# Modulation chunks of a two-layer model: four in the head, twenty multiplied on GpSimd during the even mixer

## What is computed

```
def modulate(hn, shift, scale):
    return hn * (1 + scale[:, None, :]) + shift[:, None, :]
...
proj = h @ w_in
qa, ka, va, za, ba, aa, qb, kb, vb, qi, ki, wi = split_cols(proj, EVEN_SPLITS)
...
oa = gated_delta_rule(qa, ka, va, g, beta)
...
ob = dsa_sparse_attention(qb, kb, vb, qi, ki, wi)
o = jnp.concatenate([oa.reshape(b_, s_, -1), ob.reshape(b_, s_, -1)], axis=-1)
return o @ w_out
```

## Time and profile before

| | us |
|---|---|
| median of 3 runs | 2447.55 |
| lowest and highest | 2442.32, 2449.39 |
| the profiled execution | 2446.35 |
| its span | 2444.7 |
| TensorE busy in the span | 2013.4 (82%) |
| VectorE, ScalarE busy | 647.2, 338.2 |
| GpSimd busy | 7.8 |

### The profile page before, as it was taken

The page is one execution under the profiler, slowest core; times in us unless marked ns, Lnnn a source line. Parts: engine busy times, 40 slices in busy tenths (PEclk is TensorE's granted clock), DMA queues, the critical chain, the costliest instruction groups (busy, mean ns, idle before and its releaser), DMA issues. The chain is left out here.

```text
span 2444.7 us, 28446 instructions
## 1 busy us (share of the span) xinstructions
PE 2013.4 (82%) x11842; PEld 1277.8 (52%) x11842; DVE 647.2 (26%) x1485; ACT 338.2 (14%) x690; POOL 7.8 (0%) x12
## 2 busy tenths in 40 slices
PE   1999567699999997796569999999818999789987
PEld 0374464465555553363435655555407886548753
DVE  0133653222222222103721222222231222511082
ACT  0111211100000000101211111111001121300161
POOL 0000000000000000000000000000000000000000
PEclk9799688699999998697679999999959999999989
DMA  8934001299999999932017999999873434154200
GB/s 271 386 102 165 0 2 69 102 429 427 429 428 429 429 429 403 376 105 106 1 70 303 429 429 429 429 428 429 352 266 107 143 138 142 61 124 168 98 1 26
DMA packets 154570, 590.32 MB, mean 241 GB/s; under 512 B 40784, under 2 KB 48476, under 8 KB 129668
## 3 DMA queue, kind: packets, MB, share of 16 engines
q1 hardware_dynamic: 127136, 561.63, 57.7%
q10 hardware_dynamic: 26212, 23.51, 2.9%
q0 software_dynamic: 1152, 4.19, 0.5%
HBM read 571.42 MB, written 17.89 MB: 241 GB/s over the span
## 5 line engine op out<-in xcount | busy, mean ns | idle before, releaser
L1602 PE MATMUL bank<-ring,own_tokens 128*64 128x256 f32 x4096 | 469.2, 383 | 57.0 <-DMA ring<-in_exp_w_dram 54.0
L1602 PEld LDWEIGHTS bank<-ring,own_tokens 128*64 128x64 f32 x4096 | 304.1, 138 | 238.6 <-DMA ring<-in_exp_w_dram 99.0
L506 PE MATMUL bank<-hT,ring 128*128 128x256 f32 (+1 forms) x1552 | 338.7, 381 | 5.0 <-PEq L422 5.0
L506 PEld LDWEIGHTS bank<-hT,ring 128*128 128x128 f32 (+1 forms) x1552 | 294.2, 190 | 48.6 <-issue 6.8
L1622 PE MATMUL bank<-ring,own_hiddenT 128*64 128x512 f32 x1024 | 233.8, 597 | 3.8
L495 PE MATMUL bank<-ring,hT 128*128 128x512 f32 (+2 forms) x416 | 168.8, 567 | 0.0
L1718 DVE TENSOR_TENSOR own_hidden<-bank,own_silu 128x256 f32<-128x256 f32 x64 | 27.2, 425 | 482.7 <-ACT own_silu L1662 482.7
L1581 PE MATMUL bank<-xn_kept,member 128*64 128x512 f32 x528 | 128.0, 605 | 14.1 <-issue 14.1
L1622 PEld LDWEIGHTS bank<-ring,own_hiddenT 128*64 128x64 f32 x1024 | 75.8, 136 | 120.3 <-issue 120.3
L495 PEld LDWEIGHTS bank<-ring,hT 128*128 128x128 f32 x416 | 79.0, 190 | 88.1 <-issue 83.2
L1662 ACT ACTIVATE own_silu<-bank 128x256 f32<-128x256 f32 x64 | 24.6, 384 | 680.2 <-PE bank L1602 680.2
(11 more groups left out here) (511 smaller groups left out, 1787.4 us busy)
## 6 DMA issues: line engine op xcount, KB each, us to landing
ring<-in_exp_w_dram SPq DMA_DIRECT2D x192, 2048.0 KB, 21.8
ring<-in_ada_w_dram SPq DMA_DIRECT2D x24, 2048.0 KB, 20.0
ring<-in_hawk_w_in_dram SPq DMA_DIRECT2D x15, 2048.0 KB, 8.0
expert_out<-own_out ACTq DMA_DIRECT2D x128, 128.0 KB, 8.5
ring<-in_even_w_in_dram SPq DMA_DIRECT2D x7, 2048.0 KB, 17.5
ring<-in_gla_w_in_dram SPq DMA_DIRECT2D x6, 2048.0 KB, 20.0
ring<-in_nsa_w_in_dram SPq DMA_DIRECT2D x5, 2048.0 KB, 7.9
ring<-in_even_w_out_dram SPq DMA_DIRECT2D x2, 2048.0 KB, 8.2
```

Source lines behind the costliest of these rows:

```text
L506: last = nc.tensor.matmul(pair[m // 2][0:rows, (m % 2) * T:(m % 2 + 1) * T], w[:, k, m * P:m * P + rows], src[:, k, :], start=(k == 0), st ...
L1602: last = nc.tensor.matmul(bank[2 + q][halves[half], part * FE // 2:(part + 1) * FE // 2], own[:, q, k % 4, k // 4, :], w[:, k, cols], star ...
```

## The change

The list of chunks now begins with only four modulation chunks of layer 0 (shift and scale ahead of the mixer). The other 20 (`later`) are in the list between the eight chunks of the even projections, one behind each, and twelve more behind the last. `head_stage` replaces four blocks: it issues silu(c)'s own load first, makes norm and transposes beside the products of the four chunks, and writes hT. The vectors' tables come over GpSimd's queue, the router weights are loaded by ScalarE in the projection block.

The 20 later chunks are multiplied on GpSimd in place in the ring (`ada_products`): eight multiplications by a column of silu(c), then three adds that fold eight row tiles into one, into `ada_acc` (two buffers of two chunks). GpSimd takes 8 chunks in the projections, 3 in the attention, 2 in the norms, 5 in the levels, 2 in the outputs. TensorE adds over the partitions with columns of ones (`ada_sum`), VectorE adds the bias and the gain (`ada_keep`); there are ten such sums, at the places that the diff shows. A chunk's slot is freed by GpSimd (`ada_taken`). The expert block of layer 0 has no `following` any more; SyncE fills the ring to its end there. The projection block uses three pairs of PSUM banks instead of four, since banks 6 and 7 serve the sums.

```
-            group(f"ada{layer}")
-            for j in range(12):
-                cols_of(A["ada_w"][layer], 0, KD, [(512 * j, 512)])
             if layer == 0:
-                group("even_in")
+                group("ada_first")
+                for j in range(4):
+                    ada_chunk(0, j)
+                even_at = []
                 w = A["even_w_in"][0]
+                for n, parts in enumerate([[(c0, 512)] for c0 in (0, 512, 1024, 1536, 2056, 2568, 3080)] + [[(2048, 8), (3592, 324)]]):
+                    even_at.append(len(chunks))
+                    cols_of(w, 0, KD, parts)
+                    later_at.append(len(chunks))
+                    ada_chunk(*later[n])
+                for n in range(8, len(later)):
+                    later_at.append(len(chunks))
+                    ada_chunk(*later[n])
...
+        def head_stage(rowsA, rowsB):
...
+                        act.dma_start(silu_c[:, :], flat(A["c"]).rearrange("(k p) -> p k", p=P)).then_inc(c_in.up(16), 16)
+                        act.dma_start(x[:, :, :], A["x"][0].rearrange("(t p) d -> p t d", p=P)).then_inc(x_in.up(16), 16)
+                        act.dma_start(first_gain[:, :], A["norm_mix"][0].rearrange("(k p) -> p k", p=P)).then_inc(bias_in.up(16), 16)
+                        act.dma_start(ada_bias[:, 0, 0:2, :], A["ada_b"][0, 0:2 * D].rearrange("(q k p) -> p q k", p=P, k=KD)).then_inc(bias_in.up(16), 16)
+                        act.wait_ge(c_in.sem, c_in.at(16))
+                        nc.scalar.activation(silu_c[:, :], silu_c[:, :], ACT.Silu).then_inc(silu_ready.up(), 1)
...
+                        for j in range(4):
+                            if j == 3:
+                                pe.wait_ge(consts_in.sem, consts_in.at(16))
+                                pe.wait_ge(normed.sem, normed.at(TT))
+                                turn_tiles(pe, xn, turned)
...
+        def ada_products(pool, acc, n0, n1):
+
+            for n in range(n0, n1):
+                c = later_at[n]
+                dst = acc[:, (n // 2) % 2, n % 2, :]
+                if n % 2 == 0 and n >= 4:
+                    pool.wait_ge(ada_summed.sem, n // 2 - 1)
+                arrived(pool, c)
+                w = slot(c)
+                for k in range(KD):
+                    ins = nc.gpsimd.tensor_scalar(w[:, k, :], w[:, k, :], silu_c[:, k:k + 1], None, ALU.mult)
+                for k in (4, 2):
+                    ins.then_inc(ada_steps.up(), 1)
+                    pool.wait_ge(ada_steps.sem, ada_steps.n)
+                    ins = nc.gpsimd.tensor_tensor(w[:, 0:k, :], w[:, 0:k, :], w[:, k:2 * k, :], ALU.add)
+                ins.then_inc(ada_steps.up(), 1)
+                pool.wait_ge(ada_steps.sem, ada_steps.n)
+                ins = nc.gpsimd.tensor_tensor(dst, w[:, 0, :], w[:, 1, :], ALU.add)
+                ins.then_inc(ada_taken.up(), 1)
+
+        def ada_sum(pe, acc, n, banks):
+
+            kind = later[2 * n][1] // 2
+            pe.wait_ge(ada_taken.sem, 2 * n + 2)
+            if n:
+                pe.wait_ge(ada_kept.sem, n)
...
+                                      pairs=3, tensor_work={0: turn_tables, 2: sum_kind(0), 4: sum_kind(1), 6: sum_kind(2), 7: sum_kind(3)},
+                                      scalar_work={0: load_positions, 3: sines, 4: later_loads, 6: silu_conv}, vector_work=convolve_and_rotate,
+                                      pool_work=lambda pool: ada_products(pool, acc, 0, 8), at=even_at)
...
-        def experts_stage(layer, gates, xn, gain, shift, following):
+        def experts_stage(layer, gates, xn, gain, shift):
...
-                        if following:
-                            following[2](pe)
```

More of the change, by code:

```diff
@@ L68 @@
 C_ONES = C_IDENT + P
-C_TRIU = C_ONES + P
+C_PICK = C_ONES + P
+C_EARLY = C_PICK + 1
+C_TRIU = C_EARLY
 C_LEVEL = C_TRIU + P
@@ L397, in turn_tiles @@
+        router_in, bias_in = signal("router_in"), signal("ada_bias_in")
+        consts_in, tables_in = signal("consts_in"), signal("tables_in")
+        gates = [sb(st_first, f"gates{layer}", [P, 2, D]) for layer in range(2)]
+        mod = [sb(st_first, f"mod{layer}", [P, 4, KD]) for layer in range(2)]
         def turn_tiles(pe, src, per_bank):
@@ new lines, in ada_sum @@
+        def ada_sum(pe, acc, n, banks):
[3 more added lines that the diff above has]
+                pe.wait_ge(ada_kept.sem, n)
+            whole = acc[:, n % 2, :, :].rearrange("p h n -> p (h n)")
+            for k in range(KD):
+                if kind in (2, 5):
+                    if k < 2:
+                        last = nc.tensor.matmul(banks[k][:, :], ones, acc[:, n % 2, k, :], start=True, stop=True)
+                elif kind < 2:
+                    last = nc.tensor.matmul(banks[0][:, k:k + 1], whole[:, k * P:(k + 1) * P], ones[:, 0:1], start=True, stop=True)
+                else:
+                    for half in range(2):
+                        last = nc.tensor.matmul(banks[0][half * 64:half * 64 + 64, k:k + 1], acc[:, n % 2, half, k::KD], ones[:, 0:1], start=True, stop=True)
+            last.then_inc(ada_summed.up(), 1)
@@ new lines, in ada_keep @@
+        def ada_keep(dve, n, banks):
+            layer, kind = later[2 * n][0], later[2 * n][1] // 2
+            dve.wait_ge(ada_summed.sem, n + 1)
+            dve.wait_ge(bias_in.sem, bias_in.n)
+            if kind in (2, 5):
+                for h in range(2):
+                    g = gates[layer][:, kind // 3, h * 512:(h + 1) * 512]
+                    ins = nc.vector.tensor_tensor(g, banks[h][:, :], g, ALU.add)
+                ins.then_inc(ada_kept.up(), 1)
+                return
+            half, shift = kind // 3, kind % 3 == 0
+            row = mod[layer][:, 2 * half + (1 if shift else 0), :]
+            ins = nc.vector.tensor_tensor(row, banks[0][:, 0:KD], ada_bias[:, layer, 2 * half + kind % 3, :], ALU.add)
+            if not shift:
+                ins.then_inc(vector_steps.up(), 1)
+                dve.wait_ge(vector_steps.sem, vector_steps.n)
+                gain = ffn_gain[:, layer, :] if half else col("norm_mix", 8 * layer, KD)
+                ins = nc.vector.scalar_tensor_tensor(row, row, 1.0, gain, ALU.add, ALU.mult)
+            ins.then_inc(ada_kept.up(), 1)
@@ new lines, in load_tables @@
+        def load_tables(act):
+            for layer in range(2):
+                for half in range(2):
+                    act.dma_start(gates[layer][:, half, :], A["ada_b"][layer, (3 * half + 2) * D:(3 * half + 3) * D].partition_broadcast(P))\
+                        .then_inc(bias_in.up(16), 16)
+                act.dma_start(ada_bias[:, layer, 2:4, :], A["ada_b"][layer, 3 * D:5 * D].rearrange("(q p k) -> p q k", p=P, k=KD)).then_inc(bias_in.up(16), 16)
+            act.dma_start(ada_bias[:, 1, 0:2, :], A["ada_b"][1, 0:2 * D].rearrange("(q k p) -> p q k", p=P, k=KD)).then_inc(bias_in.up(16), 16)
+            act.dma_start(ffn_gain[:, :, :], A["norm_ffn"].rearrange("l (p k) -> p l k", k=KD)).then_inc(bias_in.up(16), 16)
```

394 lines of the change are left out of this document (215 added, 179 removed).

## The result

The changed kernel takes 2508.73 us (median of 4 runs, 2505.77 to 2509.68) against 2448.47 us of the kernel before in the same comparison: a ratio of 1.0249, with a 95% interval of 1.0228 to 1.0269. It is slower by 60 us where I forecast 49 us faster, and it lies above the range. The profiled execution took 2505.77 us, its span is 2504.1 us.

A forecast was written before the change was run, and what follows sets the result against it. Even-layer blocks were taken as chains of small VectorE and TensorE steps with GpSimd idle, head and tail as held by issues and modulation work. Plus 86, minus 78, minus 57 gave minus 49: forecast 2399 us, range 2338 to 2469.

The forecast's parts named there:

- GpSimd's price, 13.8 us a chunk: Even layer's blocks: VectorE's 7.64 us times 1.8 per modulation chunk on GpSimd, 276 us in all for 20 chunks.
- the upper bound of 18.3 us: GpSimd's price: the slowest elementwise row, the scan, at 2.4 ns a column times the 7,680 columns of a chunk.
- The sign that I had named for being wrong: More than 16 us from one chunk's first product to the next one's would show the forecast wrong.
- The interference, 57 us in full: Even blocks: GpSimd stands still for VectorE instructions working all in SBUF; 31 us in projections, 7, 4, 12.7, 2.5 elsewhere.
- Rival (d): Even blocks: GpSimd binds too strongly; change loses from 16.2 us a chunk, 2469 us at 17.3; 26 in 100.
- The head, minus 78: Before the first projection: silu(c) no longer behind router loads, eight chunks fewer; projections start at 47 instead of 125 us.
- Rival (c): Head: 4 B runs go slower or silu(c) waits behind issues; head gains only 55, 2422 us; 10 in 100.
- The tail, minus 57: Behind layer 0's experts: modulation work and late SyncE issue go; norm of layer 1 starts at 968.6 instead of 1025.6 us.
- Edits at nothing: Three bank pairs, router issues in the projections (up to 37 us of ScalarE), the ring and TensorE's new waits cost nothing extra.
- The sums: Even blocks: TensorE's additions over partitions; 3 us for the last in the projections, norms' two hidden under GpSimd.
- Rival (a): Even blocks: no interference between GpSimd and VectorE; blocks plus 29 in all, 2342 us; 15 in 100.
- Rival (b): Even blocks: GpSimd near VectorE's price, 7.6 to 10 us a chunk; 2327 us; 7 in 100.

The follow-up runs named there:

- wide_mul: Changed kernel with one GpSimd multiplication of 128x4096 by spread silu(c) instead of eight of 128x512 by a column; 2465.3 us, ratio 1.0073.
- scalar_mul: Changed kernel with ScalarE making the eight multiplications of every later chunk and GpSimd only adding; 2397.3 us, ratio 0.9796.
- half_mul: Changed kernel with four of the eight GpSimd multiplications of every later chunk left out; 2398.8 us, ratio 0.9798.
- mul_only: Changed kernel without GpSimd's adds of 128x2048 and 128x1024, all multiplications and the last add kept; 2376.5 us, ratio 0.9711.
- last_add_only: Changed kernel with only GpSimd's last add of 128x512 per later chunk kept, multiplications and two adds left out; 2347.0 us, ratio 0.9587.
- scalar_small_adds: ScalarE multiplies and GpSimd adds, with the two larger adds cut into pieces of 128x512, otherwise the changed kernel; 2385.2 us, ratio 0.9756.

## Why the prediction was wrong, point by point

**GpSimd's price, 13.8 us a chunk: this step failed.** An undisturbed chunk takes 20.65 us from its start to the next one's (412.63 to 433.28 us in the levels): 12.3 us of multiplications, 6.9 and 1.3 of adds. Two things were wrong in the working. The factor 1.8 came from one tiny MEMSET; for the adds it was nearly right (4.50 against 2.29 us), but the multiplication by a column is 3.8 times VectorE's 0.43 us. And the upper bound of 18.3 us was none: the slowest elementwise row of VectorE, 2.4 ns a column, says nothing of another engine, whose own row is 3.2. Twenty times 6.85 us are 137 us. The sign that I had named for being wrong, more than 16 us from one chunk to the next, is there. The Trainium skill (GPSIMD Engine Reference, section 3, Performance versus the Vector engine) gives 4,497 ns for the add of 2,048 columns, and the trace agrees with 4,505. By the Trainium skill's factor for that add the estimate would have been 15.0 us a chunk, also too low.

**The interference, 57 us in full: wrong in size and in place.** From the first to the last instruction of each block GpSimd took 431 us for 20 chunks, 18 more than 20 x 20.65. I had let GpSimd stand still for VectorE. It is mostly VectorE that is held: its busy time in the five blocks went from 114.7 to 158.9 us, and where GpSimd works with two tensors at a time it reaches 284 (wide_mul). In the changed kernel VectorE's part costs nothing that the rows show, since GpSimd sets every block; when GpSimd gets faster, it does (the projections of wide_mul, and part of the 43 us of scalar_mul). The two errors together: 137 - 39 = 98 of the 102 us by which the even blocks were mis-forecast.

**The shape of the argument held.** Barriers throw away any slack, each block lasts as long as its share of chunks, and every microsecond a chunk counts about 20 times: half_mul took 6.2 us a chunk away, 123 us in all, and gained 110. My figure at 13.8 us a chunk was 2399 us; half_mul, at 14.5 undisturbed, took 2398.8, and mul_only, at 13.7, 2376.5. That half_mul meets the figure is luck: its interference and its waits are not those of the sum. Rival (d) was the right case, but its price (17.3 us, 2469) was too low as well. Its turning point of 16.2 us a chunk fits half_mul and mul_only on the one side and the changed kernel on the other; wide_mul, at 15.3 undisturbed and slower than before, shows that the price alone doesn't decide.

**The head, minus 78: measured minus 72.** The chain was faster than I had it: the four issues ahead of silu(c) took 0.47, 0.60, 0.49 and 4.79 us, silu(c) came at 8.64 us, not near 22, and hT was written at 40.9. What I had as two SyncE issues until 48 us lasted until 52.4, and the barrier waited 11.5 us for them alone. Rival (c), short runs of 4 B holding silu(c), is refuted.

**The tail, minus 57: measured minus 56.7.** The norm follows the last copy after 27.47 us; I had 27.3. The 27 was a choice between two merges of before, 20.2 and 28.1 us, near the one with loads beside it.

**Edits at nothing.** The router's issues took 10.8 us in the projections instead of 37 in the head and cost nothing. Three pairs of banks cost nothing that the rows show. The waits of TensorE on GpSimd are real, 28.7 and 25.6 us, but they are GpSimd's lateness, not a cost of their own:

```profile
PE bank L516 <- PEq L1194: 40.4, 1, 40.4
PE bank L510 <- POOL ada_acc L497: 28.7, 1, 28.7
PE bank L516 <- POOL ada_acc L497: 25.6, 2, 13.2
```

The sums I had at 3 us in the projections and nothing to 4 elsewhere; without GpSimd's cover the five blocks are 28 us longer in all (last_add_only), of which the sums' own rows name 8.0 in the projections. **Rival (a)**, no interference, would have given 2342 us at 13.8 us a chunk; mul_only, at that price, with little interference, took 2376.5. The 34 us are in the projections (123.3 for 113), the attention (43.9 for 41.4), the norms (32.0 for 28), the levels (85.1 for 69.5, 10.3 of it the wait for the accumulator), the outputs (31.1 for 29) and the head (52.7 for 47); what is above that sum of 40 was given back outside these blocks, and I have not traced where. **Rival (b)** fell with the price.

## What to carry to other kernels

Price work on an engine only from rows of that engine and of that kind of instruction; where there are none, a factor from another engine is a guess without an upper end, and if the change loses above a price inside the guess, that loss is a main case and no side case. Before work is moved to GpSimd beside a VectorE that works on SBUF, look for TensorE's and VectorE's own waits: here VectorE's idle time in the projections and TensorE's waits behind them took in the same twenty chunks for some 5 us more than leaving the work out. And at the end of a block with a barrier, look at the queue's last issues: with two loads that nobody needs yet moved out of the block, the kernels were 7 and 13 us faster.

## What the runs showed of the hardware

- GpSimd, float32: a multiplication of 128x512 by a column 1.65 us as recorded and 1.54 from start to start (3.2 and 3.0 ns a column), an add of two tiles 2.2 to 2.5 ns a column (1.29, 2.49 and 4.51 us for 512, 1,024 and 2,048), a multiplication of 128x4096 by a spread tile 7.07 us (1.7 ns a column). I had not expected the one with a single tensor input to cost most a column. What makes it so was not tried.
- VectorE's add of 128x512 from SBUF: 0.69 us alone, 4.87 and 4.96 us beside GpSimd's add of two tensors of 128x2048 (wide_mul, scalar_mul), 1.64 and 1.71 beside its adds of 128x512 (scalar_small_adds), 0.69 to 1.06 us beside its multiplications by a column. VectorE's copy of 128x1024: 0.69 us beside the multiplication by a column (mul_only), 7.55 beside the one of 128x4096 by a spread tile (wide_mul).
- ScalarE's multiplication of 128x512 by a column: eight in 5.0 us, beside GpSimd and VectorE at work (scalar_mul).
- A 2 MB load's issue on SyncE lasts 4.9 to 8.7 us in the head of the changed kernel, where load follows load (DMA share 1.02), and mostly 0.37 us in its projections, where the loads stand further apart (0.63). The end of the head block waited for it.
- ScalarE loads its tables 32 times in the changed kernel's expert loops (41.1 us, 1,283 ns each) and 16 times in the kernel before. The difference is the first loop, with 16 loads against none; it takes 484.7 us against 484.9 all the same. The rows show ScalarE idle ahead of these loads.
